# A tuned two-block transformer kernel on one Trainium2 core: the front of the state-space mixer in another order

## What is computed

```python
def s5_mixer(h, lam_re, lam_im, log_dt, b_re, b_im, c_re, c_im, d_skip, w_glu, b_glu):
    ...
        bu_re = jnp.einsum('blgp,gnp->blgn', u_c, bb_re)
    ...
        y = jnp.einsum('blgn,gpn->blgp', st_re, cr) - jnp.einsum('blgn,gpn->blgp', st_im, ci)
    ...
    y = (y + d_skip.astype(f32) * h.astype(f32)).astype(h.dtype)
    g = jax.nn.gelu(y)
    return g * jax.nn.sigmoid(g @ w_glu + b_glu)
```

## Time and profile before

| | us |
|---|---|
| median of 3 runs | 1377.41 |
| lowest and highest of them | 1377.22, 1378.65 |
| the profiled execution's own time | 1377.96 |
| its span, first to last instruction | 1376.3 |
| TensorE busy with matmuls | 1311.6 (95% of the span) |
| VectorE busy | 846.0 (61%) |
| ScalarE busy | 609.6 (44%) |
| mean granted TensorE clock | 0.966 of full |

### The profile page before, as it was taken

The page is one execution under the profiler, slowest core; times in us unless marked ns, Lnnn a source line. Parts: engine busy times, 40 slices in busy tenths (PEclk is TensorE's granted clock), DMA queues, the critical chain, the costliest instruction groups (busy, mean ns, idle before and its releaser), DMA issues.

```text
span 1376.3 us, 26462 instructions
## 1 busy us (share of the span) xinstructions
PE 1311.6 (95%) x11500; PEld 1225.0 (89%) x11500; DVE 846.0 (61%) x1159; ACT 609.6 (44%) x781; POOL 22.6 (2%) x32
## 2 busy tenths in 40 slices
PE   5888899999989889999999999999999999999997
PEld 4677799999966559999999999999988899999997
DVE  7895677766837646566555656446357655766543
ACT  4933553433245355444345434336343444644442
POOL 2000000000000000000000000000000000000000
PEclk9778999999999989999999999999999999999998
DMA  8953658877933843455556455454453344455452
GB/s 234 302 190 120 214 165 271 270 244 254 329 125 110 265 163 122 155 183 183 159 188 203 154 183 174 147 169 151 129 181 120 115 135 153 135 186 189 148 180 82
DMA packets 222543, 247.05 MB, mean 179 GB/s; under 512 B 5555, under 2 KB 212963, under 8 KB 222451
## 3 DMA queue, kind: packets, MB, share of 16 engines
q1 hardware_dynamic: 216178, 222.92, 50.7%
q0 software_dynamic: 5920, 22.55, 4.8%
q10 hardware_dynamic: 352, 0.23, 0.1%
HBM read 244.63 MB, written 1.05 MB: 179 GB/s over the span
## 4 chain that ended last, share of the span: by engine, by line
PE 86%; DMA 5%; DVE 4%; ACT 2%; issue 2%; SPq 1%; DVEq 0%; ACTq 0%
PE PS L1662 86%; DMA RING<-in_ada_w 3%; DMA RING<-in_ffn_w_down 1%; SPq L419 1%; DVE WL L975 1%; ACT PARTS L560 1%; DVE ARENA L995 1%; DMA RING<-in_mla_w_uq 0%; DMA RING<-in_w_in 0%; PE PS L2202 0%; DVE ARENA L1455 0%; ACT ARENA L815 0%; PE PS L2108 0%; DVE ARENA L1627 0%; DVE SQ L1631 0%
## 5 line engine op out<-in xcount | busy, mean ns | idle before, releaser
L1662 PE MATMUL PS<-PARTS 128*128 128x256 f32 (+3 forms) x3652 | 852.2, 285 | 0.0
L1662 PEld LDWEIGHTS PS<-PARTS 128*128 128x128 f32 (+1 forms) x3652 | 629.0, 190 | 1.9 <-issue 1.2
L975 DVE TENSOR_TENSOR WL<-RING,PARTS 128x2048 fp32r<-128x2048 f32 (+2 forms) x189 | 387.6, 2054 | 285.0 <-ACT PARTS L560 284.4
L1662 PE MATMUL PS<-HH,WL 128*128 128x256 f32 (+3 forms) x1832 | 525.4, 287 | 7.5 <-DVE PARTS L955 3.0
L1662 PE MATMUL PS<-HH,PARTS 128*128 128x256 f32 (+3 forms) x1832 | 523.0, 285 | 0.0
L560 ACT CAST PARTS<-RING 128x2048 fp32r<-128x2048 f32 (+2 forms) x189 | 323.7, 1715 | 311.6 <-DMA RING<-in_w_ffn_out 67.7
L1662 PEld LDWEIGHTS PS<-HH,WL 128*128 128x128 f32 (+1 forms) x1832 | 349.7, 191 | 13.3 <-issue 6.8
L1662 PEld LDWEIGHTS PS<-HH,PARTS 128*128 128x128 f32 (+1 forms) x1832 | 349.0, 190 | 0.4
L1662 PE MATMUL PS<-PARTS,WL 128*128 128x256 f32 (+1 forms) x832 | 236.9, 285 | 0.9 <-DVE WL L975 0.5
L1662 PEld LDWEIGHTS PS<-PARTS,WL 128*128 128x128 f32 x832 | 158.4, 190 | 2.4 <-issue 1.8
L1662 PE MATMUL PS<-ARENA 128*32 128x63 f32 (+8 forms) x800 | 79.7, 283 | 4.5 <-DVE ARENA L1366 2.2
(11 more groups left out here) (300 smaller groups left out, 969.7 us busy)
## 6 DMA issues: line engine op xcount, KB each, us to landing
RING<-in_w_ffn_in SPq DMA_DIRECT2D x44, 1024.0 KB, 5.1
RING<-in_ada_w SPq DMA_DIRECT2D x36, 1024.0 KB, 7.8
RING<-in_ffn_w_gate SPq DMA_DIRECT2D x22, 1024.0 KB, 5.4
RING<-in_ffn_w_up SPq DMA_DIRECT2D x22, 1024.0 KB, 5.4
RING<-in_w_in SPq DMA_DIRECT2D x20, 1024.0 KB, 5.4
ARENA<-in_ada_w POOLq DMA_DIRECT2D x12, 1024.0 KB, 7.3
RING<-in_ffn_w_down SPq DMA_DIRECT2D x16, 768.0 KB, 4.5
RING<-in_w_ffn_out SPq DMA_DIRECT2D x16, 768.0 KB, 4.2
```

The lines of the kernel that those rows point to most:

```text
L975: V.tensor_tensor(WL[:, u % SLOTS, 0:w], RING[:, u % SLOTS, 0:w], WH[:, u % SLOTS, 0:w].bitcast(fp32), SUB)\
L1662: return nc.tensor.matmul(o, lhsT, rhs, start=start, stop=stop)
```

## The change

Four things are moved or replaced, and nothing else in the kernel differs.

1. On TensorE, batch 0 goes ahead of row step 4, and batch 1 goes from behind row step 6 to behind row step 5, ahead of taps 0.
2. The skip term of taps 0 is no longer added by VectorE. ScalarE writes the identity scaled by `d_skip` into the place of the first tap matrix (eight instructions, `d_ready`), TensorE adds it to the taps in PSUM with 32 more matmuls, and ScalarE copies taps 0 out like the others (`k_out(0)`).
3. On ScalarE, `row_copy(4)` goes from ahead of the B blocks to behind C blocks 0; the scan's multiplier `RMUL` and the scaled identities stand ahead of C blocks 2; `k_out(0)` follows `row_copy(6)`.
4. On VectorE, the third C set is cut in two: its first product stays where it was, and the rest follows the first products of batch 0's rotation.

```diff
--- before.py
+++ after.py
@@ -341,7 +341,7 @@
             ada_used bu_ready prod_ready v_ready y_ready gelu_ready sig_ready
             silu_ready hid_ready kv_sq kv_stat kv_std kv_norm kr_rot kr_done hp_proj hp_sq hp_stat hp_ln hp_raw hp_std hp_scaled hp_rot hp_done
             v_copied hk_scaled hk_ready s_ready s_sb smax_ready exp_ready prob_ready pt_ready pt_copied o_ready o_copied
-            rope_sin rope_ang meta_ready qk_copied v2_copied f_act f_ready fb_ready fq_ready fb_copied fq_copied
+            rope_sin rope_ang meta_ready qk_copied v2_copied f_act d_ready f_ready fb_ready fq_ready fb_copied fq_copied
             gelu_hi w_hi w_lo norm_hi hid_hi hid_lo o_hi post_scaled rope_cos mix_sum mix_hi conv_raw conv_hi o2_hi s2_ready s2_sb s2_max s2_exp s2_prob pt2_ready pt2_copied o2_ready o2_copied
             c_copied u_ready conv_ready gate_ready mix_ready mix_part out_copied stored
             gate_scaled up_read shift_hi rc_ready rc_copied f_scaled gat_scaled yg_ready xo_ready xo_copied yo_ready row_std
@@ -713,20 +713,24 @@
             bt_out(2)
             bt_out(3)
             shift(0, ADA_SHIFT1)
-            row_copy(4)
             b_blocks(None)
             act.wait_ge(S["turn_cos"], 1)
             nc.scalar.activation(by_pair(SIN), by_pair(COS), ACT.Sin, scale=2 * PI_IN)
             link(nc.scalar.activation(by_pair(COS), by_pair(COS), ACT.Abs))
             nc.scalar.activation(by_pair(COS), by_pair(COS), ACT.Sin, scale=-TWO_PI, bias=hpi).then_inc(S["turn_sin"], 1)
             c_blocks(0)
+            row_copy(4)
             c_blocks(1)
             row_copy(5)
-            c_blocks(2)
             nc.scalar.activation(RMUL[:, :, 1:], R4[:, 0, :].unsqueeze(2).broadcast_to([P, PAIRS, NCH - 1]), ACT.Copy)
             nc.scalar.activation(RMUL[:, :, 0:1], R4[:, 0, :].unsqueeze(2), ACT.Copy, scale=0.0).then_inc(S["r_ready"], 1)
+            for kt in range(KT):
+                ins = nc.scalar.activation(KW4[0][:, kt, :], ident, ACT.Copy, scale=vec("s5_d", kt))
+            ins.then_inc(S["d_ready"], 1)
+            c_blocks(2)
             c_blocks(3)
             row_copy(6)
+            k_out(0)
             for d in range(1, CHUNK):
                 row_copy(6 + d)
                 k_out(d)
@@ -1220,14 +1224,18 @@
             link(V.tensor_tensor(f, f, RMUL[:, :, :], ADD))
             V.tensor_scalar(f, f, 0.5, -0.5, ALU.min, ALU.max).then_inc(S["turn_cos"], 1)
 
+            def c_first(k):
+
+                V.tensor_tensor(CIM[:, :, :, :], by_channel(WPOW, 1, k), CRE[:, :, :, :], MUL)
+
             def c_set(k):
 
                 a = CSET[:, 2 * (k % 2):2 * (k % 2) + 2, :, :]
                 t = CIM[:, :, :, :] if k < 3 else CSET[:, 0:2, :, :]
                 if k >= 1:
                     dve.wait_ge(S["c_pow"], k)
-                if k < 3:
-                    V.tensor_tensor(t, by_channel(WPOW, 1, k), CRE[:, :, :, :], MUL)
+                if k < 2:
+                    c_first(k)
                 if k >= 2:
                     dve.wait_ge(S["ct_exp"], k - 1)
                 ins = V.tensor_tensor(a, by_channel(WPOW, 0, k), CRE[:, :, :, :], MUL)
@@ -1240,8 +1248,10 @@
 
             dve.wait_ge(S["ct_used"], 1)
             dve.wait_ge(S["bt_ready"], 2 * CHUNK)
-            for k in range(3):
+            for k in range(2):
                 c_set(k)
+            dve.wait_ge(S["c_pow"], 2)
+            c_first(2)
 
             def turned_in(kt):
 
@@ -1286,12 +1296,8 @@
             dve.wait_ge(S["bd_zero"], 1)
             for kt in range(4):
                 turned_in(kt)
+            c_set(2)
             c_set(3)
-            dve.wait_ge(S["k_ready"], 1)
-            for kt in range(KT):
-                at = kt % 4 * P
-                ins = V.scalar_tensor_tensor(KW4[0][:, kt, :], ident, vec("s5_d", kt), PS[:, 5 + kt // 4, at:at + P], MUL, ADD)
-            ins.then_inc(S["k_used"], 1)
             for kt in range(4):
                 turned(kt)
             for kt in range(4):
@@ -1965,7 +1971,7 @@
                 if d == 0:
                     pe.wait_ge(S["late_loaded"], 16)
                     pe.wait_ge(S["norm_std"], 1)
-                    pe.wait_ge(S["tr_used"], 1)
+                    pe.wait_ge(S["d_ready"], 1)
                     for b in (5, 6):
                         mm(PS[:, b, :], CN[:, C_MASK + P:C_MASK + 2 * P], CN[:, C_ID:C_ID + 512], True, True)
                 else:
@@ -1975,7 +1981,10 @@
                         for q in range(4):
                             rows = slice(32 * q, 32 * q + 32)
                             c0 = kt % 4 * P + 32 * q
-                            ins = mm(PS[rows, 5 + kt // 4, c0:c0 + 32], BD[:, i, 4 * kt + q, :], CT4[d][i][:, kt, rows], i == 0, i == 1)
+                            o = PS[rows, 5 + kt // 4, c0:c0 + 32]
+                            ins = mm(o, BD[:, i, 4 * kt + q, :], CT4[d][i][:, kt, rows], i == 0, d > 0 and i == 1)
+                            if d == 0 and i == 1:
+                                ins = mm(o, KW4[0][:, kt, rows], ident[:, rows], False, True)
                 ins.then_inc(S["k_ready"], 1)
 
             def y_of(kt):
@@ -1995,16 +2004,16 @@
                                      t == CHUNK - 1 and i == 1)
                 ins.then_inc(S["y_ready"], 1)
 
-            ada_rows(4)
             for kt in range(4):
                 b_u(kt)
+            ada_rows(4)
             ada_cols(4)
             ada_rows(5)
+            for kt in range(4, KT):
+                b_u(kt)
             taps(0)
             ada_cols(5)
             ada_rows(6)
-            for kt in range(4, KT):
-                b_u(kt)
             for d in range(1, CHUNK):
                 ada_cols(5 + d)
                 ada_rows(6 + d)
```

## The result

| | before | changed |
|---|---|---|
| median of 20 runs, us | 1377.17 | 1382.80 |
| lowest, highest | 1371.21, 1380.33 | 1371.09, 1391.09 |
| ratio, 95% interval | | 1.0043 (1.0025 to 1.0062) |
| the profiled execution's own time | 1377.96 | 1379.41 |
| its span | 1376.3 | 1377.7 |

The changed kernel is slower by 5.6 us by the medians (0.41%), by 0.43% by the ratio. The forecast was 1378.3 with a range up to 1382.3; the result lies half a microsecond above it. The two profiled executions differ by 1.4 us only: executions of one program spread over 9 to 20 us, so a pair of profiles shows how the work lies, not what the change costs.

The account below looks back on a forecast made before the run. The prediction took TensorE's own work, issue gaps and clock to bound the front. Start 0, +1.8 us by taps 1 and -0.9 later gave +0.9, so 1378.3 us, range 1373.9 to 1382.3.

Parts of the forecast that it names:

- What bounds the front, and the counted points: TensorE's own work, issue gaps and clock bound the front; gaps come at multiples of 127 matmul records, as program fetches.
- Start and batch 0: TensorE's batch 0 starts near 54.0 us, after ScalarE's first shift, and ends near 66.6, taking 11.6 to 13.3 us.
- ScalarE isn't late for it: ScalarE reaches row step 4's copy in time, behind C blocks 0; only the bare copy with handover, 0.7 us, is paid.
- The sign given for it: Before the outputs, a TensorE wait for VectorE or ScalarE of over 1 us would show the prediction wrong.
- Batch 1, columns to row step 7: Batch 1 from 73.2 to 86.5 us without a wait, then taps 0, columns and row steps; taps 1 start at 97.9.
- Taps 1 to the outputs: TensorE's 18.4 us stretch: two or three gaps of 1 to 2.5 us replace one of 4.65; -0.9 us, bounds -4 and +3.
- the one on SyncE's queue: Loads for row step 6 are issued at 69.6 us instead of 55; at worst a microsecond is waited.
- The skip term: In taps 0 on TensorE, 32 more matmuls, 64 records at 10 ns each, add 0.65 us; upper bound 2.0 us.
- Off the path: VectorE's fourth C set is done near 84.5 us and its last state at 122.5, some 2 us late, hidden by slack.
- Low clock spreads: Rival: idle 1.5 us before batch 0 drops TensorE's clock, which stays low through later steps; +5.5 us, 1382.9, chance 0.22.
- Gaps thinned: Rival: with batch 1 next to batch 0 prefetch keeps up and the 4.65 us gap goes; -4 us, 1373.5, chance 0.15.
- products set the pace: Rival: batch 1's earlier release is what TensorE lacks, so 5 us come off; 1372.4, chance 0.03.

Follow-up runs that it names:

- e11: The changed kernel run again without any edit, for a second profile: 1.0051 of the kernel before.
- e13: The changed kernel with ScalarE's copy of row step 4 ahead of C blocks 0 instead of behind them: 1.0053 of the kernel before.
- e1: The changed kernel with row step 4 and its copy back ahead of batch 0: 1.0015 of the kernel before.
- e17: The same program as e1, run again: 1.0015 of the kernel before, median 1378.64 us.
- e3: The changed kernel with TensorE's whole old order, keeping the new skip term with what it needs of ScalarE's and VectorE's order: 1.0017 of the kernel before.
- e8: The kernel before with the gate's ring loads held until the fourth output and the two clearing matmuls moved from taps 0 ahead of row step 4: 1.0009.
- e6: The kernel before with 32 short matmuls, all into the same 32 columns, added ahead of the front: 1.0019 of the kernel before.
- e9: The kernel before with 32 short matmuls on rotating quarters of the array, into changing places, added ahead of the front: 1.0012 of the kernel before.

## Why the prediction was wrong, by its own steps

- **What bounds the front, and the counted points: right.** Between the gaps from 78.4 on stand 127, 380 (three times 127), 127, 127 and 127 records, and every point of the tap blocks stood where it was foretold, within ten records.
- **Start and batch 0: near.** 54.0 to 66.6 foretold; 55.17 to 67.8 measured, with 1.0 us of it in untouched code. The repeat took 8.3 us for batch 0, outside the bounds of 11.6 to 13.3, so the agreement of the first trace is in part luck. Row step 4 and its copy took 3.9 us to columns 4, foretold 3.7.
- **"ScalarE isn't late for it": wrong, and harmless.** It holds only if batch 0 meets the low clock. In e11 it was late by 4.96 us. But e13 removed this and stayed at 1.0053. The sign given for it, a wait of TensorE for ScalarE of over 1 us, couldn't tell: the prediction itself foretold 1.5 us of idle time for the shift ahead of batch 0, and 1.55 came.
- **Batch 1, columns to row step 7: right as a sum.** Taps 1 began at 98.88, or 97.8 with the 1.0 us of untouched code taken off; 97.9 was foretold. Two errors cancelled in it: the two clearing matmuls ran at the low clock (3.78 us for 1.99), and the following steps took 6.4 us where 7.5 were given.
- **"Taps 1 to the outputs", −0.9: wrong in this trace, by +5.5.** From 98.88 to 121.88 are 23.0 us, against 18.4. The mechanism, "two or three gaps of 1 to 2.5 us", was right in kind, but there were four and they sum to 8.6 us instead of 4.65. The outputs then gave 2.2 us back (20.8 for 23.0 us). Yet e1 and e17, with batch 1 in the same place, took 23.5 and 24.1 us for the same stretch (93.43 to 116.90, 99.09 to 123.18) and measured 1.0015, so this term isn't the price either.
- **The step that failed, as far as the runs show, is the one on SyncE's queue:** "55 becomes 69.6 ... so at worst a microsecond is waited." The times were right (69.75) and so was the absence of a wait, but the price was read from the consumer's wait alone. With nothing else moved, late loads raised the ratio from 1.0015 to 1.0045 and 1.0046, 0.0030 or 4.1 us, where the sum has nothing. By what mechanism, and where in the execution, stays open.
- **The skip term is the second, as a size:** 0.65 us given; 0.0017 of 1377, 2.3 us, measured in e3, the orders on ScalarE and VectorE that go with it included. Its interval, -0.0001 to 0.0034, holds the 0.65 us too. The rest of the forecast's +0.9 was +1.3 for row step 4, its copy and the steps up to batch 1, -0.2 for the steps ahead of taps 1 and -0.9 for the later part. The two measured prices, 4.1 + 2.3 = 6.4 us, are of the size of the whole, 5.9 by the ratio of the changed kernel (0.0043) and 7.0 by that of its repeat (0.0051).
- **Off the path: right.** VectorE's last state at 122.4, foretold 122.5; C set 4 done at 84.5, foretold 84.5; the 1.0 us by which this trace began late is in both.
- **The rivals.** "Slower" had a chance of 0.26, "the same" 0.54. "Low clock spreads" gave 1382.9, which is nearly the result, but that is luck: the stretch began at 56.7, behind the point that it named, ended at 70.4, and the four stretches summed to 34.1 us for 34.2. That idle time alone brings the low clock isn't borne out: it began anywhere from 56.7 to 68.1 behind the same 1.55 us. "Gaps thinned" and "products set the pace" didn't happen. No change lies outside the interval of the measured ratio.

## What to carry to other kernels

When a step is moved, list the buffers that it releases and when the loads into them will now run, and test their lateness by itself even if the consumer never waits. Here two loads of 1 MB held back by some 11 us stood at 0.3% more with nothing else changed, and taking four other loads out of the busy stretch gave 0.2% back; the mechanism isn't known, so these are figures of this kernel. Where TensorE stops at counted places of its program, ask which one limits the next stretch before counting a gain: 2 us taken off ahead of one (e8) came back as a gap of 4.76 us. And repeat both a variant and its reference before a difference of 0.3% is believed: two profiles of the same program differed by 6.3 us in where the outputs began (e1, e17), while the ratios of repeated programs agreed within 0.001.

## What the runs showed of the hardware

- 32 matmuls over the whole array into one and the same 32 columns took 13.28 us for 62 records (0.21 us each, e6). The same number on quarters of the array, into changing places, took 0.76 us for 64 records (0.012 us each, e9). Two things differ between them, and which of them costs the time wasn't tested.
- The gaps at counted places don't keep a fixed distance. In the changed kernel they came 6.7 us (103.42 to 110.14), 6.5 (to 116.60) and 3.8 (to 120.43) after each other, with 127 records in each stretch.
- The same program met the low clock from 56.7 us in one execution and from 68.1 in another, and ran batch 0 in 12.65 and 8.3 us.
